# A layer of GLA, Hyena and SwiGLU on one core: the order of its lead-in and the placing of the w_ada products

## The reference

```python
sh1, sc1, g1, sh2, sc2, g2 = split(silu(c) @ w_ada + b_ada, 6)      # w_ada: 2048 x 12288
csh1, csc1, ...            = split(silu(c_ctx) @ w_ada + b_ada, 6)
hc = rmsnorm(ctx, norm_pre_mix) * (1 + csc1) + csh1
s_f, s_b = context_states(hc, w_in, ...)        # keys, values, decays of the context
hx = rmsnorm(x, norm_pre_mix) * (1 + sc1) + sh1
# mixer: z = hx @ w_in, split into q, k, v, decays, g, zh, mg
#   o    = chunked gated linear attention, both directions, from s_f, s_b
#   y_hy = gated long convolution by FFT; its filters are a small sine MLP times a window
#   out  = (sigmoid(mg_a) * (o @ p_gla) + sigmoid(mg_b) * (y_hy @ p_hy)) @ w_out
x  = x + g1 * rmsnorm(mixer(hx), norm_post_mix)
hx = rmsnorm(x, norm_pre_ffn) * (1 + sc2) + sh2
x  = x + g2 * rmsnorm((silu(hx @ ffn_gate) * (hx @ ffn_up)) @ ffn_down, norm_post_ffn)
```

## Time and profile before

| | us |
|---|---|
| median of 3 runs (1802.09 to 1806.05) | 1804.81 |
| profiled execution, its own time | 1803.66 |
| its span | 1801.9 |
| PE busy | 1672.7 |
| DVE busy | 1103.6 |
| ACT busy | 727.2 |

### The profile page before, as it was taken

One profiled execution on the slowest core, in us unless ns is written; L12 is line 12 of the kernel. 1 busy time (PEld: TensorE's weight loads), 2 busy tenths in 40 slices (PEclk: granted clock), 3 DMA queues, 4 the chain that ended last, 5 costly groups with the idle time before them and its releaser, 6 DMA issues.

```text
span 1801.9 us, 22810 instructions
## 1 busy us (share of the span) xinstructions
PE 1672.7 (93%) x8614; PEld 1359.7 (75%) x8614; DVE 1103.6 (61%) x1286; ACT 727.2 (40%) x830; POOL 76.8 (4%) x147
## 2 busy tenths in 40 slices
PE   3799998999989679989998969999999999899998
PEld 1456676788877458778886858888888888788886
DVE  3635564577786766876996585555555555455545
ACT  2212225533343122444442365555555554344444
POOL 0000000000001101110010000000000000000000
PEclk9999999999998789999998989999999999999999
DMA  6857746566658758988888745565566556455553
GB/s 226 287 172 262 243 136 197 163 203 192 190 156 288 231 188 272 299 269 262 275 272 289 237 137 188 190 192 188 186 189 192 189 186 189 160 193 192 194 191 128
DMA packets 263713, 378.12 MB, mean 210 GB/s; under 512 B 13685, under 2 KB 222976, under 8 KB 262048
## 3 DMA queue, kind: packets, MB, share of 16 engines
q1 hardware_dynamic: 242784, 296.19, 51.1%
q0 software_dynamic: 20336, 80.36, 13.4%
q10 hardware_dynamic: 528, 0.67, 0.1%
HBM read 372.99 MB, written 4.19 MB: 209 GB/s over the span
## 4 chain that ended last, share of the span: by engine, by line
PE 75%; DVE 10%; DMA 10%; issue 3%; ACT 2%; ACTq 0%; POOL 0%; DVEq 0%; SPq 0%; POOLq 0%
PE ps L1306 27%; PE ps L1307 14%; DMA a2raw<-in_w_ada 9%; PE ps L1314 9%; PE ps L1316 8%; PE ps L1315 8%; DVE acc L977 2%; DVE lo L863 2%; PE ps L1267 2%; PE ps L1257 1%; PE ps L1461 1%; DMA cp<-k_pack 1%; PE ps L1437 1%; PE ps L1388 0%; PE ps L1452 0%
## 5 line engine op out<-in xcount | busy, mean ns | idle before, releaser
L863 DVE TENSOR_TENSOR lo<-raw,hi 128x1024 fp32r<-128x1024 f32 x488 | 593.4, 1221 | 363.8 <-ACT hi L690 299.2
L1306 PE MATMUL ps<-hx,hi 128*128 128x512 f32 x1408 | 489.0, 394 | 2.5 <-DVE lo L863 2.4
L1306 PE MATMUL ps<-hxc,hi 128*128 128x512 f32 x1088 | 411.7, 419 | 46.5 <-DVE lo L863 46.5
L690 ACT ACTIVATE hi<-raw 128x1024 fp32r<-128x1024 f32 x260 | 275.2, 1060 | 330.0 <-PE ps L1307 197.7
L1307 PE MATMUL ps<-hx,lo 128*128 128x256 f32 x1408 | 390.1, 277 | 0.0
L508 ACT ACTIVATE hi<-raw 128x1024 fp32r<-128x1024 f32 x224 | 235.9, 1058 | 321.9 <-PE ps L1307 165.1
L1307 PE MATMUL ps<-hxc,lo 128*128 128x256 f32 x1088 | 313.4, 288 | 0.0
L1306 PEld LDWEIGHTS ps<-hx,hi 128*128 128x128 f32 x1408 | 264.0, 188 | 64.8 <-DVE lo L863 3.4
L1306 PEld LDWEIGHTS ps<-hxc,hi 128*128 128x128 f32 x1088 | 215.2, 198 | 109.8 <-DVE lo L863 43.4
L1307 PEld LDWEIGHTS ps<-hx,lo 128*128 128x128 f32 x1408 | 264.4, 188 | 0.0
L1307 PEld LDWEIGHTS ps<-hxc,lo 128*128 128x128 f32 x1088 | 216.1, 199 | 1.7 <-issue 1.4
(11 more groups left out here) (265 smaller groups left out, 1619.9 us busy)
## 6 DMA issues: line engine op xcount, KB each, us to landing
raw<-in_w_in SPq DMA_DIRECT2D x160, 512.0 KB, 4.9
a2raw<-in_w_ada POOLq DMA_DIRECT2D x128, 512.0 KB, 5.1
raw<-in_ffn_gate SPq DMA_DIRECT2D x88, 512.0 KB, 3.4
raw<-in_ffn_up SPq DMA_DIRECT2D x88, 512.0 KB, 3.5
raw<-in_ffn_down SPq DMA_DIRECT2D x88, 512.0 KB, 3.6
ada_raw<-in_w_ada SPq DMA_DIRECT2D x64, 512.0 KB, 4.7
raw<-in_w_out SPq DMA_DIRECT2D x32, 512.0 KB, 5.2
raw<-in_p_gla SPq DMA_DIRECT2D x16, 512.0 KB, 4.7
```

Of the source, the lines that this page charges most:

```text
L690: nc.scalar.activation(hi[:, slot, :], raw[:, uu % RING, :], ACT.Copy).then_inc(hi_done, 1)
L863: V.tensor_tensor(lo[:, uu % RING, :], raw[:, uu % RING, :], hi[:, uu % 4, :].bitcast(f32), SUB).then_inc(lo_done, 1)
L1306: mm(bank(b), hi[:, uu % 4, c0:c0 + P], feat[:, k, :], start=first, stop=False)
```

## The change

In the lead-in, PE no longer waits for the whole constants (`s_const`); the `fwd` part is loaded by POOL. ACT squares the first two tiles ahead of the first sine and takes the root ahead of the third. `filt` is gone: all eight filter products are `filter_part`s in the gaps of blocks 0 and 1, all eight spectra in block 2. The strips go between the sines on PE, the first weight tile is loaded ahead of the fourth strip, and its low half is cut between DVE's two normalising passes. The modulation for the next block is placed behind piece 9 (block 0), 8 (block 1) and 7.

The order of the w_ada parts is now 3, 2, 4, 5. Part 3 is spread over units 27 to 102, part 2 over 110 to 148, part 4 over 162 to 211, and part 5 over the first eight passes of the FFN loop. Its row sum follows the twelfth unit of the last pass, where DVE adds b_ada; `grow * acc` is made just ahead of the output. Part 4's column sum stands behind unit 223, in the place of the row sum. POOL's other loads keep their conditions and now stand between other halves. DVE's FFN loop is written out for the first eight passes and the last, PE's for the last.

```diff
-        outw = at("outw", O_A2, [HID, D])
+        outw = at("outw", O_RC + 24 * KB, [HID, D])
...
-                  ("onorm", 2, 82, "d"), ("onorm", 3, 84, "d"), ("uturn", 0, 87, "pa"),
-                  ("red", 0, 89, "pd")]
-        STEPS += [("dft", i, 93 + 5 * i, "pd") for i in range(4)]
-        STEPS += [("red", 1, 110, "pd"), ("idft", 0, 114, "pd"), ("idft", 1, 118, "pd"),
-                  ("cut", 0, 124, "d"), ("cut", 1, 130, "d"), ("red", 2, 150, "pd"),
-                  ("row", 0, 154, "d")]
+                  ("onorm", 2, 82, "d"), ("onorm", 3, 84, "d"), ("uturn", 0, 87, "pa")]
+        STEPS += [("dft", i, 93 + 5 * i, "pd") for i in range(3)]
+        STEPS += [("red", 0, 106, "pd"), ("dft", 3, 108, "pd"), ("idft", 0, 114, "pd"),
+                  ("idft", 1, 118, "pd"), ("cut", 0, 124, "d"), ("cut", 1, 130, "d"),
+                  ("red", 1, 152, "pd"), ("row", 0, 158, "d")]
...
-        A2_CHUNK = [3, 4, 2, 5]
-        A2_AT = ([27 + int(1.8 * a) for a in range(32)] + [92 + int(0.5 * a) for a in range(32)]
-                 + [112 + int(1.1 * a) for a in range(32)] + [158 + int(1.95 * a) for a in range(32)])
+        A2_CHUNK = [3, 2, 4, 5]
+        A2_AT = ([27 + int(2.45 * a) for a in range(32)] + [110 + int(1.25 * a) for a in range(32)]
+                 + [162 + int(1.6 * a) for a in range(32)])
...
-        AFTER = [{2: "a", 4: "a", 3: "t", 7: "a", 9: "a", 10: "c"} for _ in range(2)]
+        AFTER = [{1: "a", 3: "at", 5: "a", 8: "a", 9: "c"}, {0: "a", 1: "at", 3: "a", 6: "a", 8: "c"}]
         AFTER += [{0: "a", 1: "at", 2: "a", 5: "a", 7: "c"} for _ in range(NB - 3)] + [{}]
-        SPEC_AFTER = {1: {0: 0, 3: 1, 5: 2, 8: 3}, 2: {0: 4, 3: 5, 6: 6, 8: 7}}
-        FILT_AFTER = {0: {0: 0, 2: 1, 4: 2, 6: 3}}
+        MOD_AT = [9, 8] + [7] * (NB - 3)
+        FILT_AFTER = [{1: 0, 4: 1, 7: 2, 10: 3}, {0: 4, 2: 5, 4: 6, 6: 7}] + [{}] * (NB - 2)
+        SPEC_AFTER = {0: 0, 1: 1, 2: 2, 3: 3, 4: 4, 6: 5, 8: 6, 10: 7}
...
-            sp.dma_start(cp[:, K_ID:K_ONE + P], k_pack[:, K_ID:K_ONE + P]).then_inc(s_id, 16)
+            for c0, c1 in ((K_ID, K_ONE + P), (K_SEL, K_END)):
+                sp.dma_start(cp[:, c0:c1], k_pack[:, c0:c1]).then_inc(s_id, 16)
...
-            for n in range(4):
+            for n in range(3):
                 ada_load(n)
-            for uu in range(3):
-                weight_load(uu)
+            weight_load(0)
+            ada_load(3)
+            weight_load(1)
+            weight_load(2)
...
+            pool.dma_start(cp[:, K_FWD:K_SEL], k_pack[:, K_FWD:K_SEL]).then_inc(s_fwd, 16)
...
-            for a in range(32):
+            for a in range(25):
                 a2_load(a)
             for e in "pda":
                 pool.wait_ge(x_sem[e], upto(STEPS, e, stepno("onorm", 3)))
...
             pool.dma_start(kk2[:].rearrange("p a b n -> p (a b n)"), kk_dram).then_inc(s_kkl, 16)
             pool.dma_start(inv[:], k_inv.rearrange("k p n -> p k n")).then_inc(s_inv, 16)

-            for a in range(32, 64):
+            for a in range(25, 34):
                 a2_load(a)
             pool.wait_ge(x_sem["d"], upto(STEPS, "d", stepno("dft", 3)))
             pool.dma_start(grow[:], b_ada[:, 2 * D:3 * D].broadcast_to([P, D])).then_inc(s_row[0], 16)
-            for a in range(64, 96):
+            for a in range(34, 64):
                 a2_load(a)
-            pool.wait_ge(x_sem["p"], upto(STEPS, "p", stepno("red", 2)))
+            pool.wait_ge(x_sem["p"], upto(STEPS, "p", stepno("red", 1)))
             pool.dma_start(acc[:], n_post_mix.broadcast_to([P, D])).then_inc(s_row[1], 16)
-
-            for a in range(96, 116):
+            for a in range(64, 87):
                 a2_load(a)
             pool.wait_ge(ev_dve, N_GRP["w"][0])
             pool.dma_start(x1[:], x.rearrange("(t p) n -> p t n", p=P)).then_inc(s_x1, 16)
-
-            for a in range(116, 128):
+            for a in range(87, 96):
                 a2_load(a)
             pool.wait_ge(j_dve, 4)
             pool.dma_start(grow[:], b_ada[:, 5 * D:6 * D].broadcast_to([P, D])).then_inc(s_row[2], 16)
+
+            for a in range(96, 128):
+                a2_load(a)
...
             start_step("turn")
+            square(0)
+            square(1)
             start_step("sine", 0)
-            square(0)
-            start_step("sine", 1)
-            square(1)
-            start_step("sine", 2)
             square(2)
             square(3)
+            start_step("sine", 1)
             nc.scalar.activation(st[:, 4:8], st[:, 0:4], ACT.Sqrt, bias=eps[:, 0:1],
                                  scale=1.0 / D).then_inc(s_rms, 1)
+            start_step("sine", 2)
+            cut_high(0)
             rows(0)
             modulate(0)
             modulate(1)
-            for uu in range(3):
-                cut_high(uu)
+            cut_high(1)
+            cut_high(2)
...
+                if b == 2:
+                    for m in range(3):
+                        spectrum(m)
...
                     cut_high(3 * b + 5)
-                if b == 1:
+                if b == 2:
                     spectrum(3)
+                    spectrum(4)
                 if b < NB - 1:
                     rows(b + 1)
+                    if b == 2:
+                        spectrum(5)
+                    modulate(2 * b + 2)
+                    modulate(2 * b + 3)
+                if 0 < b < NB - 1:
+                    cut_high(3 * b + 5)
                 if b == 2:
                     spectrum(6)
...
+                if j == 0:
+                    act.wait_ge(j_mod, 1)
...
+            def filter_part(m):
+
+                i, cols = m // 4, slice(512 * (m // 2 % 2), 512 * (m // 2 % 2 + 1))
+                if m == 0:
                     dve.wait_ge(s_win, 32)
-                    V.tensor_tensor(filt_f[:], bank(0, 2), win[:, 0, :], MUL)
-                    link(V.tensor_tensor(filt_b[:], bank(2, 2), win[:, 0, :], MUL))
-                    link(V.memset(filt_b[0:1, :], 0.0))
-                    V.tensor_tensor(filt_e[:, 0, :], filt_f[:], filt_b[:], ADD)
-                    V.tensor_tensor(filt_o[:, 0, :], filt_f[:], filt_b[:], SUB).then_inc(done, 1)
-
-            def filter_part(m):
-
-                cols = slice(512 * (m // 2), 512 * (m // 2 + 1))
                 dve.wait_ge(flt_pe, m + 1)
-                ins = V.tensor_tensor((filt_f, filt_b)[m % 2][:, cols], bank(7), win[:, 1, cols], MUL)
+                ins = V.tensor_tensor((filt_f, filt_b)[m % 2][:, cols], bank(7), win[:, i, cols], MUL)
                 if m % 2 == 0:
                     ins.then_inc(flt_dve, 1)
                     return
                 link(ins)
-                V.tensor_tensor(filt_e[:, 1, cols], filt_f[:, cols], filt_b[:, cols], ADD)
-                V.tensor_tensor(filt_o[:, 1, cols], filt_f[:, cols], filt_b[:, cols], SUB
+                if m == 1 or m == 3:
+                    link(V.memset(filt_b[0:1, cols], 0.0))
+                V.tensor_tensor(filt_e[:, i, cols], filt_f[:, cols], filt_b[:, cols], ADD)
+                V.tensor_tensor(filt_o[:, i, cols], filt_f[:, cols], filt_b[:, cols], SUB
                                 ).then_inc(flt_dve, 1)

             def normalize(cols):
...
+            unit_low(0)
             normalize(slice(256, D))
-            start_step("filt")
             columns(0)
...
+                    if idx in ((3, 6, 8) if b == 0 else (1, 5, 10)):
+                        unit_low(3 * b + 3 + idx // 4)
+                    if b < NB - 1:
+                        if idx == MOD_AT[b]:
+                            columns(b + 1)
+                        if idx in (MOD_AT[b] + 1, MOD_AT[b] + 2):
+                            features(2 * b + 1 + idx - MOD_AT[b])
...
-                    elif 32 <= a < 96:
-                        dve.wait_ge(x_sem["p"], upto(STEPS, "p", stepno("red", a // 32 - 1)))
+                    elif 32 <= a < 64:
+                        dve.wait_ge(x_sem["p"], upto(STEPS, "p", stepno("red", 0)))
+                    elif 64 <= a < 96:
+                        dve.wait_ge(x_sem["d"], upto(STEPS, "d", stepno("row")))
                     elif a >= 96:
-                        dve.wait_ge(x_sem["d"], upto(STEPS, "d", stepno("row")))
+                        dve.wait_ge(j_cols, 1)
                     V.tensor_scalar(dst, src, cs[:, 0, 0:1], None, MUL).then_inc(a2_done, 1)
...
-            dve.wait_ge(j_pe, 1)
-            dve.wait_ge(s_row[2], 16)
-
-            V.tensor_tensor(grow[:], bank(0, 4), grow[:], ADD).then_inc(f_up, 2)
+            dve.wait_ge(j_cols, 1)
+            link(V.tensor_tensor(modc[:, 4, :], bank(0)[:, 0:KD], col1[:, B_SC2:B_SC2 + KD], ADD))
+            V.scalar_tensor_tensor(modc[:, 4, :], modc[:, 4, :], 1.0, col1[:, N_FFN:N_FFN + KD], ADD,
+                                   MUL).then_inc(j_mod, 1)
             dve.wait_ge(j_act, 4)
...
+                    if t == k == 0:
+                        ins.then_inc(f_dve, 1)
...
```

(72 more changed lines are left out.)

124 lines of the change are left out of this document (48 added, 76 removed).

## The result

The changed kernel takes 1761.9 us, median of four runs (1755.28 to 1763.86), against 1803.45 (1801.62 to 1806.05) for the kernel before: 0.976 of its time, 95% interval 0.973 to 0.979. The profiled execution took 1761.38 us, its span is 1759.5. So the change gains 42 us where 54 were forecast, inside the range. All terms but one came within 4 us of their forecast. The one that failed lies where the sum had put nothing: the 176 gate and up units of the FFN. The 1803.45 is itself a low draw of four: all 51 executions of the kernel before, those beside the experiments included, lie between 1797.9 and 1817.5 with a median of 1806.7, so the 3.6 us that the prediction took as the smallest difference it could tell is too small.

A forecast was written before the change was run, and what follows sets the result against it. It took PE products as the largest shares, with removable waits of DVE and PE for transfers, chiefly w_ada halves. Stage terms summed to -53.7 from 1803.7, giving 1750 us; the range was 1733 to 1767.

The forecast's parts named there:

- blocks 3 to 7, units to 86: Blocks 3 to 7 and the units to 88 keep their order: nothing gained or lost.
- p units: DVE is the limit there; groups of four units take 11.98 us with 2.5 halves each: +7.5 us, bounds +3 and +10.
- FFN start: Column sum hides in PE's wait for `xn`; the product on `grow` moves to the end: -1.8 us.
- Lead-in: Up to the first block product, which comes near 41.8 us instead of 55.76: gain 14, bounds 10 and 17.
- First three blocks: More filter products +4.5, less idle -5.8, left idle +1.2, clock -2: -2 us in all, bounds -5 and +2.
- First w_ada part: Near unit 88, half 25 waits behind `kk2` and `inv`, PE stalls 10 us: net +6 us, bounds 0 and +9.
- Units 93 to 158: Two terms: -41 us (bounds 36 and 43) where 32 halves were due, then -9 us (bounds -15 and -1).
- Rival B: Each half keeps 4.0 us wherever halves are due, so the load pace follows the halves: 1762 us; chance 0.17.
- Reload of x: PE's wait of 6.98 us behind x falls one unit later, about 4 us idle: -3 us, bounds -5 and 0.
- FFN: Gate and up units at 2.78 us each; the 32 halves in the first eight passes cost nothing, bound +3.
- Rival E: Slower than before: 32 halves in the first eight FFN passes cost 2.9 us each, 92 in all: 1842 us; chance 0.03.
- Row sum: Four row-sum products, hidden before, now lie between two units of the last FFN pass: +3.6 us.

The follow-up runs named there:

- e1_lead: The kernel before with only the lead-in and block part of the change; 1789.7 us, 0.987 of the kernel before.
- e2_kk: The changed kernel with two more w_ada halves (25 and 26) loaded ahead of POOL's wait for the heads and `kk2`; 1747.3 us.
- e6_grow: The changed kernel with the load of `grow` moved from between halves 33 and 34 to behind half 63; 1756.3 us.
- e3_x1: The changed kernel with the reload of x moved from between halves 86 and 87 to behind half 95; 1748.3, 1757.3, 1748.7 and 1757.7 us.
- e4_none: The changed kernel without the 32 w_ada halves in the FFN, loads and accumulation both (last gate row wrong); 1757.2 us.
- e12_base: The kernel before with two-column-group products ordered high, high, low, low and nothing else changed; 1807.0 us.
- e10_pairs: The changed kernel with products ordered high, high, low, low wherever a unit multiplies two column groups; 1755.5 us.
- e8_probe: The changed kernel with FFN passes written out on PE and extra products of ten sorts inserted at 20 places in ten passes; 1766.2 us.
- e9_order: The changed kernel with FFN passes 1 to 9 written out on PE, six in three other product orders; units of 2.773, 2.787, 2.79 and 2.793 us.
- e11_best: The changed kernel with four edits (`kk2`, `grow` and x loaded later, part 4's new pace) and products high, high, low, low; 1723.7 us, 0.953 of before.
- e7_all: The changed kernel with four edits: `kk2` behind half 26, `grow` behind 63, x behind 95, part 4's new pace; 1729.3 us, 0.957 of before.

## Why the prediction was right, point by point

The difference of unit ends between the two profiled executions, stage by stage (us, minus is earlier):

| step of the sum | forecast | measured |
|---|---|---|
| lead-in, to the first block product | -14 | -13.95 |
| first three blocks | -2 | +1.9 |
| blocks 3 to 7, units to 86 | 0 | -2.6 |
| first part's end, units 86 to 93 | +6 | +8.0 |
| units 93 to 110 | -41 | -40.9 |
| units 110 to 158 | -9 | -9.3 |
| p units | +7.5 | +6.2 |
| reload of x, w_out | -3 | -1.6 |
| FFN start | -1.8 | -1.5 |
| FFN's units | 0 | +8.9 |
| row sum in the last pass | +3.6 | +3.5 |
| behind it | 0 | -1.1 |
| sum | -53.7 | -42.4 |

**Lead-in.** Every link of the chain came where it was worked out: context squares from 21.37 (21.4), the second sine 25.44 to 25.86 (26.0), DVE done with the third leg at 30.28 (30.4), normalising over at 38.6, modulation at 39.55 (39.5), the product at 41.81 (41.8). e1_lead shows that it stands alone. The cover that the prediction called about gone was gone: PE could start on the fourth strip at 34.77, its columns were made by 38.99, and normalising was over at 38.6, so the strip, not DVE, came last by 0.4 us. The four strips and the first tile were there at 34.8, where the sum had 37.6: it took 292 GB/s from a stretch late in the kernel, while the lead-in of before ran at 357 over 27 us and at 401 over 15 (windows of before):

```profile
3.00:30.00 27.00, 4.17 (x8) 1.23 (x8) 6.40 (x22) 5.53 (x7) 0.00 (x0) 1.00 1.02 357
6.00:21.00 15.00, 2.00 (x4) 0.65 (x4) 1.39 (x9) 1.54 (x2) 0.00 (x0) 1.00 1.02 401
```

The 358 GB/s that the prediction quotes as a limit was therefore none for this core. With its own 37.6 and the 4.2 us from there to the columns the first product would have come near 44.6, an estimate from these rows; that the sum named 41.8 is luck on this link. A table load took 1.28 us, as the sum had it, and the next activation followed at once (load from 25.87, activation from 27.17), so the 2.66 us that the prediction names beside its sum didn't show.

**First three blocks.** Wrong sign, by 3.9. PE's work grew by the 4.5 of filter products as forecast. Too large was what idle time would give back: PE stands idle 2.23 and 0.69 us at the second block and 1.24 at the third,

```profile
73.86 0.50 PE L1325 MATMUL ps<-hi,hxc 128*128 128x512 f32 x1 [2.23 <-DVE hxc L847]
...
75.52 0.49 PE L1325 MATMUL ps<-hi,hxc 128*128 128x512 f32 x1 [0.69 <-DVE hxc L847]
...
106.20 0.50 PE L1325 MATMUL ps<-hi,hxc 128*128 128x512 f32 x1 [1.24 <-DVE hxc L847]
```

4.2 in all, where 1.2 was left. Modulation stands earlier, but at the second block DVE does a filter part, 2.7 us, between it and the features (70.08 to 72.66), and at the third a low half, 1.2 us, between the two features. The clock gave 1.4 in place of 2: 7.0 us at half clock between 41.8 and 142.1, 9.7 before.

**First w_ada part.** Right in place, cause and sign. DVE stopped at unit 88 for half 25; the half's add ended at 545.2, PE waited 11.0 us (10 forecast). The clock fell while PE still waited, at 540.3, and 4.1 us of its 10.2 at half speed lay behind the wait:

```profile
546.41:550.53 4.12, 4.12 (x13) 3.54 (x14) 4.05 (x7) 0.00 (x0) 0.53 (x1) 0.50 0.57 142
```

They cost 2.1 us (2.5 forecast). From unit 88 to 93 after lost 6.4 us on before, so the term of +6 is right; the other 1.6 of the +8.0 are not its own. They belong to the 2 us that units 80 to 86 had gained: PE stood 1.3 us for a low half in unit 87, and from 79 to 88 the two kernels took 37.3 and 37.6 us. e2_kk shows the cause of the long wait alone.

**Units 93 to 158.** Both terms right, and the wait behind `grow` among them: 4 forecast, 3.6 measured, 5.5 with its clock (e6_grow). Of the 7 us of loss that the sum left to this stage the other 3, taken from a load pace of 4.0 us a half, didn't come: apart from unit 113, from 0.6 us at unit 134 and from the steps behind 114, 118 and 152 the units 110 to 158 ran at 2.77 or 2.83 with 31 halves in them. In place of the 3 stood 1.3 more at unit 113, the 0.6, and 1.2 from the slower 2.83 in 22 units, so that the term fits to 0.3 us is in part luck. Rival B, which asked for that load pace everywhere, is out.

**p units.** DVE sets the pace, as worked out, but halves come whole: groups took 11.4 us with two of them and 13.1 to 13.8 with three, where the sum had 11.98 for each. The 6.2 us are the excess of the three long groups; of the 2.3 for the lead that the row product takes, nothing shows. Timeline of DVE, the first operation of four evacuations:

```profile
827.60 0.68 DVE L942 TENSOR_TENSOR pa<-ps,evc 128x512 f32<-128x512 f32 x1
...
838.97 0.69 DVE L942 TENSOR_TENSOR pa<-ps,evc 128x512 f32<-128x512 f32 x1
...
852.03 0.68 DVE L942 TENSOR_TENSOR pa<-ps,evc 128x512 f32<-128x512 f32 x1
...
863.41 0.69 DVE L942 TENSOR_TENSOR pa<-ps,evc 128x512 f32<-128x512 f32 x1
```

**Reload of x.** It moved by one unit as forecast, and PE waited 6.4 us in place of 7.0; the forecast of 4 was too low. e3_x1 shows that the 2 MB of x are the cause; why they stop PE for 6.4 and not 4 is not shown.

**FFN.** Rival E is out: with the halves left out (e4_none) the pace stays. "FFN: nothing" was right for the halves and wrong for the stage. The prediction took 2.78 us for a unit as the measure of a full stream and never asked whether the stream has a second pace, though the trace of before shows it: units 120 to 127 and 188 to 190 there took 2.83, units 153 to 186 2.77. Windows of 20 us in the two, in before:

```profile
721.00:741.00 20.00, 20.00 (x115) 17.33 (x114) 15.23 (x14) 9.70 (x11) 2.86 (x5) 1.00 0.91 288
845.00:865.00 20.00, 20.00 (x117) 17.48 (x116) 14.81 (x17) 10.00 (x12) 1.60 (x3) 1.00 0.87 280
```

This is the step that failed; it is worth 8.9 of the 11.3 us by which the sum missed, and it needs nothing of the change: e1_lead has it with the old FFN, e3_x1 lacks it with the new one, and where both kernels have one pace the change measures 51.5 (e12_base, e10_pairs) against the 53.7 forecast. Whether the change makes the slow pace more likely isn't known: with the FFN of before one profiled execution had it and one hadn't, with the new FFN and the old order seven had it and two hadn't.

The other misses, from +3.9 to -2.6, add up to 2.4; that they cancel so far is luck.

**Row sum.** Between two units of the last pass, in the open:

```profile
1490.26 3.60 PE L1596 MATMUL ps<-acc,cp 128*128 128x512 f32 x8
```

## What to carry to other kernels

Where one queue issues transfers in a written order, look for each wait in it at what is queued behind and when that is due; here three such places cost 12, 8.5 and 5.5 us, and moving one line each removed them without a new wait. Sum a change stage by stage from the ends of the units and compare at the same points afterwards: a miss then has an address. Count a half clock only where it lies behind the wait: what falls into the wait costs nothing. And before a difference below 1% is put down to an edit, look whether a stage that the edit didn't touch runs at the same pace in both traces, and whether single executions of one kernel lie that far apart.

## What the runs showed of the hardware

**Two rhythms of one stream.** A stream of products that alternate 512 and 256 columns, each with new weights, ran at full clock in one of two rhythms. In after (timeline of PE; the low products between them left out) the pattern repeats every three pairs, 1.06 us:

```profile
1299.81 0.40 PE L1317 MATMUL ps<-hx,hi 128*128 128x512 f32 x1
...
1300.16 0.40 PE L1317 MATMUL ps<-hx,hi 128*128 128x512 f32 x1
...
1300.52 0.40 PE L1317 MATMUL ps<-hx,hi 128*128 128x512 f32 x1
...
1300.87 0.40 PE L1317 MATMUL ps<-hx,hi 128*128 128x512 f32 x1
```

and in e3_x1 every two, 0.69 us:

```profile
1299.80 0.39 PE L1315 MATMUL ps<-hx,hi 128*128 128x512 f32 x1
...
1300.14 0.39 PE L1315 MATMUL ps<-hx,hi 128*128 128x512 f32 x1
...
1300.49 0.39 PE L1315 MATMUL ps<-hx,hi 128*128 128x512 f32 x1
```

That is 353 or 347 ns for a pair, 2.827 or 2.773 us for a unit, 9.4 us over the FFN. The rhythm held as long as the stream did (over 470 us here), and in e8_probe it changed at foreign products only: at 12 of the 20 insertions, and once more at the row sum behind unit 395. Of the eleven profiled executions with the old order three began the FFN in the fast one (before, e3_x1, e9_order) and eight in the slow one. What decides is open: the last stop ahead of it was 1.57 us in before (fast) and 1.62 in e1_lead (slow), and of the ten sorts of insertion in e8_probe, used twice each, eight gave each rhythm once and two gave the slow one twice. The Trainium skill, TensorE: Matmul & The Clock Gate, section "Back-to-back issue gap", gives N / 2.4 + 2.5 ns for a warm product alone, which makes an estimate of 325 ns for such a pair, and for a long stream of 512 columns a lower figure than for one alone; no run here came under 346 ns a pair.

**The order of equal work sets the pace.** High, high, low, low took 2.787 us a unit in every profiled execution that had it (e9_order in two passes, e10_pairs, e11_best, e12_base): 0.5% over the fast rhythm, 1.4% under the slow one, and the spread of the executions shrank with it, from 15.7 to 1.8 us in e11_best against e7_all, from 15.5 to 7.5 in e12_base against the kernel before. Why the order has one pace is not shown.

**The clock behind a column sum.** The pace of the FFN isn't the whole of the spread: 19.6 us over the 51 executions of before is twice the 9.4. One more source can be seen at one place. Behind unit 106 PE makes the column sum (32 products of one column, about 4 us) without standing idle. In after the granted clock then fell to half (1.2 GHz) for 6.8 us, in e3_x1, e8_probe and e10_pairs for 3.4, and in e7_all not at all, and unit 107 with the sum took 9.17, 7.9 and 6.35 us. Windows around it in after and in e7_all:

```profile
605.00:622.00 17.00, 17.00 (x90) 14.90 (x89) 7.63 (x9) 4.43 (x6) 0.00 (x0) 0.80 0.43 123
590.00:606.00 16.00, 16.00 (x104) 14.28 (x103) 9.69 (x13) 5.56 (x7) 0.53 (x1) 1.00 0.51 142
```

PE was busy throughout both. What decides between the three is open.
